# Banded attention of a two-block transformer: 64x64 scores on array halves, a standing mask in PSUM, query and gate tiles paired per step

## The reference

```python
def sink_softmax(sc, sink):
    m = jnp.maximum(jnp.max(sc, axis=-1, keepdims=True), sink)
    e = jnp.exp(sc - m)
    return e / (jnp.sum(e, axis=-1, keepdims=True) + jnp.exp(sink - m))
...
    valid = jnp.concatenate([jnp.ones((NC, N_META), dtype=bool),
                             jnp.repeat(band_chunk >= 0, CHUNK, axis=1)], axis=1)
    sr = jnp.einsum('bnqkgd,bnskd->bnkgqs', qr, kb).astype(jnp.float32) * scale
    sr = jnp.where(valid[None, :, None, None, None, :], sr, -jnp.inf)
    pr = sink_softmax(sr, sink[None, None, :, :, None, None])
    orr = jnp.einsum('bnkgqs,bnskd->bnqkgd', pr.astype(v.dtype), vb).reshape(B, S, D_MODEL)
...
def swa_layer(x, norm_g, w_in, w_out, sinks, k_sh, v_sh, cos, sin):
    B, L, _ = x.shape
    q, gate = jnp.split(rms_norm(x, norm_g) @ w_in, 2, axis=-1)
    q = partial_rope(q.reshape(B, L, B_Q_HEADS, B_HEAD_DIM), cos, sin)
    o = swa_sink_attention(q, k_sh, v_sh, sinks)
    return x + (o * jax.nn.silu(gate)) @ w_out
```

## Time and profile before

| | us |
|---|---|
| three runs | 3123.31, 3130.84, 3141.76 (median 3130.84) |
| the profiled execution's own time | 3129.51 |
| its span | 3127.7 |

### The profile page before, as it was taken

The page is one execution under the profiler, slowest core; times in us unless marked ns, Lnnn a source line. Parts: engine busy times, 40 slices in busy tenths (PEclk is TensorE's granted clock), DMA queues, the critical chain, the costliest instruction groups (busy, mean ns, idle before and its releaser), DMA issues.

```text
span 3127.7 us, 58205 instructions
## 1 busy us (share of the span) xinstructions
PE 2875.6 (92%) x23908; PEld 2721.0 (87%) x23908; DVE 950.0 (30%) x1275; ACT 1166.1 (37%) x1302; POOL 1898.5 (61%) x786
## 2 busy tenths in 40 slices
PE   6999999988898899899898989899988999999997
PEld 6889998987777678799788888899988999999996
DVE  3322232153212211221436363632514213031222
ACT  3433344333333333354424242424334434343442
POOL 4565666655343337466636364647874888888784
PEclk9999999998888779899999999999998999999998
DMA  4444444433232225454434343435653666666563
GB/s 165 134 134 117 138 146 123 140 117 110 80 95 71 70 74 176 127 150 135 138 96 127 96 127 96 122 109 156 196 174 103 188 183 188 189 180 189 177 188 116
DMA packets 119996, 425.21 MB, mean 136 GB/s; under 512 B 12672, under 2 KB 18944, under 8 KB 119552
## 3 DMA queue, kind: packets, MB, share of 16 engines
q1 hardware_dynamic: 115104, 416.53, 44.8%
q10 hardware_dynamic: 4704, 5.77, 0.6%
HBM read 418.05 MB, written 4.19 MB: 135 GB/s over the span
## 4 chain that ended last, share of the span: by engine, by line
issue 38%; PE 33%; POOL 26%; DVE 2%; ACT 0%; POOLq 0%; DMA 0%; DVEq 0%; ACTq 0%; SPq 0%
POOL wl L2085 26%; PE ps L216 9%; PE ps L223 9%; PE ps L214 9%; PE ps L234 2%; PE ps L1403 1%; DVE og L329 1%; PE ps L1832 0%; PE ps L1839 0%; PE ps L1834 0%; DVE xT L321 0%; ACT wh L195 0%; POOLq L2088 0%; DVE hl L1867 0%; DVE arena L315 0%
## 5 line engine op out<-in xcount | busy, mean ns | idle before, releaser
L2085 POOL TENSOR_TENSOR wl<-raw,wh 128x1024 fp32r<-128x1024 f32 x782 | 1898.3, 2449 | 1195.1 <-ACT wh L195 1194.4
L195 ACT ACTIVATE wh<-raw 128x2048 fp32r<-128x2048 f32 x391 | 747.4, 1912 | 842.0 <-PE ps L223 491.8
L214 PE MATMUL ps<-hh,wh 128*128 128x256 f32 (+1 forms) x3568 | 906.0, 291 | 54.1 <-DVE hl L257 42.8
L216 PE MATMUL ps<-hl,wh 128*128 128x256 f32 (+1 forms) x3568 | 898.9, 289 | 0.0
L214 PEld LDWEIGHTS ps<-hh,wh 128*128 128x128 f32 x3568 | 689.8, 193 | 61.0 <-issue 43.8
L216 PEld LDWEIGHTS ps<-hl,wh 128*128 128x128 f32 x3568 | 692.0, 194 | 0.7
L223 PE MATMUL ps<-hh,wl 128*128 128x256 f32 (+1 forms) x3568 | 469.8, 284 | 0.0
L223 PEld LDWEIGHTS ps<-hh,wl 128*128 128x128 f32 x3568 | 449.0, 190 | 0.2 <-POOL wl L2085 0.2
L214 PE MATMUL ps<-gh,wh 128*128 128x256 f32 x1536 | 395.2, 295 | 0.3 <-ACT wh L195 0.3
L216 PE MATMUL ps<-gl,wh 128*128 128x256 f32 x1536 | 389.7, 292 | 0.0
L214 PEld LDWEIGHTS ps<-gh,wh 128*128 128x128 f32 x1536 | 310.3, 202 | 3.0 <-ACT wh L195 0.5
(11 more groups left out here) (296 smaller groups left out, 2450.5 us busy)
## 6 DMA issues: line engine op xcount, KB each, us to landing
raw<-weights SPq DMA_DIRECT2D x782, 512.0 KB, 3.6
xT<-tokens SPq DMA_DIRECT2D x1, 2176.0 KB, 8.6
spill<-xT ACTq DMA_DIRECT2D x1, 2048.0 KB, 7.5
xT<-spill ACTq DMA_DIRECT2D x1, 2048.0 KB, 10.0
out<-xT SPq DMA_DIRECT2D x1, 2048.0 KB, 7.5
C<-consts SPq DMA_DIRECT2D x1, 1984.0 KB, 12.0
arena<-lora ACTq DMA_DIRECT2D x4, 384.0 KB, 3.1
P<-params SPq DMA_DIRECT2D x1, 125.0 KB, 12.8
```

Source lines behind the costliest of these rows:

```text
L195: nc.scalar.activation(wh[:, m % 2, :, :].rearrange("p a b -> p (a b)"), raw[:, 2 * (m % 2):2 * (m % 2) + 2, :, :].rearrange("p a b c -> p ...
L214: nc.tensor.matmul(acc[0:m, 0:n], wh[:, slot, kt, 0:m], rh[:, kt, 0:n], start=(kt == kts[0]), stop=False)
L216: nc.tensor.matmul(acc[0:m, 0:n], wh[:, slot, kt, 0:m], rl[:, kt, 0:n], start=False, stop=False)
L2085: nc.gpsimd.tensor_tensor(wl[:, s // 2, h, :], raw[:, s, :, :], wh[:, s // 2, h, :].bitcast(F32), ALU.subtract)\
```

## The change

- **Scores.** Each head's 64 queries of a chunk are multiplied with exactly the keys that they may see, on half the array: weights 64 x 64 (one chunk of queries of one head), five column ranges (80, 144, 208, 16 and 192 keys) for each of the two heads, ten products a step. Queries of even chunks go to partitions 0 to 63 of the output, of odd chunks to 64 to 127; head a writes bank 2 + a. Keys lie with the meta keys first.
- **Mask.** The places of banks 2 and 3 that no product writes are filled with -1e30 once, by five VectorE fills before the loop. The mask products and the zeroed key array go; `kd` is one copy of the keys in each half.
- **Values.** `turn_kv` turns the values in blocks of 64 keys into both halves of the partitions, 20 products, after the first query tile.
- **Steps.** 16 steps, all written out, each with one query tile (of the next step) and one gate tile; the gate tile is cut into six parts (`part`), four ahead of the transposes and two behind. Eight transposes instead of ten; one ScalarE copy `wx` and one VectorE copy `w2` take the turned weights out of PSUM. P·V is five blocks of keys for each head, ten products of 64 x 64 weights. The output bank alternates (4 + s % 2), as do q and gb.
- **Rotation** of the queries: 256 columns per step, between the scaling of the probabilities and the copy `w2`.
- **Split** of the outputs: three quarters inside the steps 5 to 14, the fourth behind.
- The order of weight tiles in DRAM follows.

```diff
+        def part(pe, phase_name, t, k, acc, rh, rl, n):
+            q = FIRST[phase_name] + t
+            slot = q % 2
+            if k == 0:
+                pe.wait_ge(hi_done, q + 1)
+            if k < 4:
+                for kt in range(4 * k, 4 * k + 4):
+                    nc.tensor.matmul(acc[:, 0:n], wh[:, slot, kt, :], rh[:, kt, 0:n], start=(kt == 0), stop=False)
+                    ins = nc.tensor.matmul(acc[:, 0:n], wh[:, slot, kt, :], rl[:, kt, 0:n], start=False, stop=False)
+            else:
+                pe.wait_ge(lo_done, 2 * q + k - 3)
+                for kt in range(8 * (k - 4), 8 * (k - 4) + 8):
+                    ins = nc.tensor.matmul(acc[:, 0:n], wl[:, slot, kt, :], rh[:, kt, 0:n], start=False,
+                                           stop=(kt == 15))
+            return ins
...
+        f2 = carve([("pair", PAIR), ("kd", 4, NT), ("v2", 5, 256), ("q", 2, 256), ("sh", 256), ("xc", 256),
+                    ("p0", 6, 64), ("p1", 10, 64), ("wx", 512), ("w2", 512), ("gb", 2, 256), ("stb", 32),
+                    ("kv", 4, NT), ("ksh", 2, NT)])
...
-            nc.vector.memset(fb["kd"], 0.0)\
-                .then_inc(V.sem, V.step("zero"))
-            dve.wait_ge(V.sem, V.at("zero"))
-            for g in range(4):
-                for h in range(2):
-                    nc.vector.tensor_copy(fb["kd"][64 * h:64 * h + 64, g, NT * h:NT * h + NT],
-                                                 fb["kv"][64 * (g % 2):64 * (g % 2) + 64, g // 2, :])\
-                        .then_inc(V.sem, V.step(f"k{g}_{h}"))
+            dve.wait_ge(SK["a"].sem, SK["a"].at("c3"))
+            for k, (rows, at) in enumerate((((0, 128), (0, 48)), ((0, 128), (192, 240)), ((0, 64), (128, 192)),
+                                          ((0, 64), (448, 512)), ((64, 128), (256, 320)))):
+                nc.vector.memset(ps[rows[0]:rows[1], 2:4, at[0]:at[1]], NEG)\
+                    .then_inc(V.sem, V.step(f"neg{k}"))
+            dve.wait_ge(V.sem, V.at("radd"))
+            for h in range(2):
+                for e in range(2):
+                    to = kd[64 * h:64 * h + 64].rearrange("p (a b) n -> p a b n", b=2)[:, :, e, :]
+                    of = x[64 * e:64 * e + 64]
+                    nc.vector.tensor_copy(to[:, :, META:NT], of[:, :, 0:SEQ])\
+                        .then_inc(V.sem, V.step(f"k{h}{e}"))
+                    nc.vector.tensor_copy(to[:, :, 0:META], of[:, :, SEQ:NT])\
+                        .then_inc(V.sem, V.step(f"m{h}{e}"))
...
+            for b in range(5):
+                keys = slice(64 * b - 64, 64 * b) if b else slice(NT - 64, NT)
+                for k in range(2):
+                    for a in range(2):
+                        at = 256 * (b % 2) + 128 * k
+                        ins = mm(ps[64 * a:64 * a + 64, 4 + b // 2, at:at + 128], kv[:, 2 + k, keys], c("ident"))
...
+            for s in range(STEPS_B):
+                g, ends = s // 4, s == STEPS_B - 1
+                pe.wait_ge(SQ["v"].sem, SQ["v"].at("radd", s))
+                if s:
+                    pe.wait_ge(A.sem, A.at("e3", s - 1))
+                halves = [(slice(64 * a, 64 * a + 64), 2 + a) for a in range(2)]
+                for rows, at, keys, to in ((slice(0, 64), 0, slice(0, 80), 48), (slice(64, 128), 64, slice(0, 144), 48),
+                                           (slice(0, 64), 128, slice(0, 208), 240),
+                                           (slice(64, 128), 192, slice(0, 16), 240),
+                                           (slice(64, 128), 192, slice(80, 272), 240)):
+                    for r_, b in halves:
+                        ins = quad(ps[rows, b, to + keys.start:to + keys.stop], q[r_, s % 2, at:at + 64],
+                                   kd[r_, g, keys])
...
+                if not ends:
+                    pe.wait_ge(SQ["a"].sem, SQ["a"].at("q", s))
+                    tile(pe, "b", 1 + 2 * s, 0, 0, [(ps[:, 0, :], gh, gl, ALL)], SEQ).then_inc(tile_done, 1)
+                if s:
+                    pe.wait_ge(A.sem, A.at("g", s - 1))
+                n = 2 + 2 * s - ends
+                for k in range(4):
+                    part(pe, "b", n, k, ps[:, 1, :], gh, gl, SEQ)
+
+                pe.wait_ge(V.sem, V.at("p3", s))
...
+                for k in (4, 5):
+                    ins = part(pe, "b", n, k, ps[:, 1, :], gh, gl, SEQ)
...
+                pe.wait_ge(A.sem, A.at("wx", s))
+                pe.wait_ge(V.sem, V.at("w2", s))
+                if s >= 2:
+                    pe.wait_ge(V.sem, V.at("o", s - 2))
+                o = ps[:, 4 + s % 2, 0:256]
+                for b, cols, w_ in ((0, slice(0, 256), w2[:, 256:512]), (1, slice(0, 256), wx[:, 0:256]),
+                                    (2, slice(0, 256), wx[:, 256:512]), (3, slice(128, 256), w2[:, 0:128]),
+                                    (4, slice(128, 256), w2[:, 128:256])):
                     for a in range(2):
+                        r_ = slice(64 * a, 64 * a + 64)
+                        ins = quad(o[r_, cols], v2[r_, b, 64 * g:64 * g + 64], w_[r_, :], start=(b == 0),
+                                   stop=(b == 4))
...
+            for s in range(STEPS_B):
+                ends = s == STEPS_B - 1
+                act.wait_ge(V.sem, V.at("sn", s))
...
+                nc.scalar.activation(stb[:, B_SN:B_SN + 4], stb[:, B_SN:B_SN + 4], ACT.Exp)\
+                    .then_inc(A.sem, A.step("es"))
+                if not ends:
+                    query(s + 1)
+                if s in (5, 9, 13):
+                    split_bo.quarter_act(act, SB["v"], SB["v"].at("o", s - 2), s // 4 - 1)
+                act.wait_ge(T.sem, T.at("wt", s))
+                nc.scalar.activation(f2["wx"], ps[:, 6, :], ACT.Copy)\
+                    .then_inc(A.sem, A.step("wx"))
+                n = 2 + 2 * s - ends
+                act.wait_ge(tile_done, done("b", n))
+                if s >= 2:
+                    act.wait_ge(V.sem, V.at("o", s - 2))
+                nc.scalar.activation(f2["gb"][:, s % 2, :], ps[:, 1, 0:256], ACT.Silu)\
+                    .then_inc(A.sem, A.step("g"))
+                round_weights(act, "b", n + 2)
...
+                for k in range(4):
+                    w_ = (p0 if k < 2 else p1).rearrange("p (b a) n -> p b a n", a=2)[:, :, k % 2, :]
+                    nc.vector.tensor_scalar(w_, w_, stb[:, B_RR + k:B_RR + k + 1], None, ALU.mult)\
+                        .then_inc(V.sem, V.step(f"p{k}"))
+                if s < STEPS_B - 1:
+                    rope(s + 1)
+                dve.wait_ge(T.sem, T.at("wt", s))
+                nc.vector.tensor_copy(f2["w2"], ps[:, 7, :])\
+                    .then_inc(V.sem, V.step("w2"))
+                if s in (6, 10, 14):
+                    split_bo.quarter_dve(dve, s // 4 - 1)
+                dve.wait_ge(T.sem, T.at("pv", s))
+                dve.wait_ge(A.sem, A.at("g", s))
```

326 lines of the change are left out of this document (114 added, 212 removed).

## The result

| | before, us | after, us |
|---|---|---|
| runs on the same chip, median (lowest to highest) | 3133.52 (3123.31 to 3141.76), 4 | 2968.61 (2966.87 to 2970.47), 4 |
| profiled execution, span | 3127.7 | 2964.6 |
| first scores | 735.99 | 715.44 |
| attention stage, first scores to the end of the last P·V | 406.2 | 267.9 |
| first accumulation of the output product | 1151.80 | 990.47 |

The ratio is 0.9446, with a 95% interval of 0.9396 to 0.9495 (the quotient of the two medians, 0.9474, lies inside it): 165 us less. The forecast of 2966 us and its range hold.

A forecast was written before the change was run, and what follows sets the result against it. TensorE's work in the banded attention, partly at half clock, was taken as the bound. First scores 718.7, cold start 3, steps 261 and tail 5.9 gave 988.6 against 1151.8: 163 us off 3129.5, forecast 2966 us, range 2936 to 3008.

The forecast's parts named there:

- The front: Before the attention stage: key copies, value copy and first rotation put first scores at 718.7 us (712 to 722), saving 17.
- cold first step: First step of the attention stage: 3 us more for a fallen clock.
- A step without a wait: One attention step of TensorE: scores 1.3, tiles 5.6 and 3.75, transposes 0.9, last third 1.9, P·V 1.9; 15.3 us.
- VectorE's queue: Attention steps: GpSimd holds the rotation, delaying the turned-weights copy and P·V by 0 to 2.6 us; 1.0 taken, 16.3 a step.
- Rival 1: Attention steps: VectorE is never late, 15.3 us a step, 245 us for the steps, 2947 us in all; chance 0.20.
- The clock: Attention steps: P·V and scores together for 3.2 us, not 9.3; fallen clock costed at nothing while no wait is added.
- Rival 2: Attention steps: the clock falls each step after wait and small work, 18.5 us a step, +35, 3001 us; chance 0.20.
- The sum: Up to the output product: 718.7 + 3 + 261 + 5.9 = 988.6 against 1151.8 us, 163 us saved.
- Tail: From the end of P·V to the output product's first accumulation: 5.9 us instead of 9.7, only the last quarter's split waiting.
- Rival 3: Scores and P·V: array halves don't run together, scores +1.2, P·V +1.9, 49 us in all, 3015 us; chance 0.05.
- 4: Attention steps: switching between full array and halves lets nothing overlap, 30.2 us a step, +217, 3183 us; chance 0.03.
- my "four": Attention steps on TensorE: changing the tiling mode drains the array, four times a step; no time given.

The follow-up runs named there:

- the mask experiment: The kernel before without the six mask products of a step, the mask left out of the computation: stage 306.2 us instead of 406.2, ratio 0.976.

## Why the prediction was right, and where it was right by two errors

- **The front.** 718.7 forecast, 715.44 measured. The key copies were caught by GpSimd four times, as said (2.38, 2.36, 2.53 and 2.32 us), but the value copy was done at 712.99, and the rotation behind it was held for 0.99 us once, not to the end of the next two instructions. Most of the 3.3 us is no merit of the sum: VectorE began its fills at 699.99 instead of the 702.5 taken from the profile of before, and when the kernel was profiled again the first scores came at 717.97. The turning of the values took 2.40 us; I had 4.3, "half if halves run together". The cold first step cost 2.3 against 3.
- **A step without a wait.** 15.3 forecast, 14.88 measured. The mis-sized term is the scores: 1.3 against 0.96. Tile, transposes, last third and P·V (1.91) came as taken.
- **VectorE's queue.** The mechanism and its size stand: held product, held sum, copy behind them, 2.4 us instead of 2.6, in seven of fifteen steps. The average of 1.0 a step was taken between the bounds and came out as 1.1, a guess that was met; that the late step lets the next escape was the reason given, and it is what the periods show. Rival 1 (never late) is the kernel with the rotation through PSUM: its stage of 241 stands near the 245 given for it.
- **The clock.** This step failed. I costed it at nothing "while no wait is added", and then added a wait of 2.6 us to every second or third step without costing the clock again. In six of the seven late steps P·V and the scores behind it ran at half clock in part; 10 us. Rival 2 had the mechanism, and overpriced it at 2.2 us for all 16 steps.
- **The sum.** 261 + 3 for the stage against 267.9: steps too long by 0.4 times 15, or 6 us, and a missing 10 for the clock. The stage was right to 4 us because the two errors have opposite signs, and this miss and the front's cancel again: the end of P·V was forecast for 982.7 (718.7 + 3 + 261) and came at 983.38.
- **Tail.** 5.9 forecast, 7.1 measured; the last quarter took VectorE 2.31 us, beside GpSimd, and I had 1.2; TensorE waited 0.9 us for it.
- **Rival 3** (halves don't run together, +49) and **4** (switching lets nothing overlap, +217) fall: P·V 1.91 and scores 0.96 are below the values that rest on the earlier trace rows. The rule of the Trainium skill, "TensorEngine Tiling (Array Packing)", Key Properties, that a change of the tiling mode drains the array, I weighed against the change; it spoke for it, if for anything. In the rows of the kernel before shown with the mask experiment, products of 128 rows and masks of one row alternate in the scores: two mask records between others take 0.36 us (866.08 to 866.44), four take 0.59 (867.09 to 867.68), so a record takes 0.115 and what is left, 0.13, is a cost of each group of masks, however many it holds. The trace fits the rule so far, but doesn't prove it. The removed masks made eight of them a step, the new halves make two (as the order in the kernel has it), since P·V and the next scores stand together (my "four" was a miscount). Whether the 0.13 us is a drain or a load of weights that nothing hides, no run here tells apart.
- **What the prediction didn't see** is that a part of the change it named in half a sentence, the mask, carries most of the gain: 100 us, against 165 in all. The steps' sum held it without telling: 5.8 us of scores and 1.8 of cold tile went out together.

**To carry to other kernels.** Price small matmuls by records, not columns, and add what their stretch does to the clock: the masks, of 64 columns each, cost some 39 us by themselves and 61 through the clock. Before a VectorE queue that TensorE waits for is placed beside a busy GpSimd, give its operations on two tensors an operand in PSUM, or put the one that TensorE waits for ahead of those that can be held. And when a wait is added to a sum, cost the clock after it again.

## What the runs showed of the hardware

- Two operations of 256 columns took 0.43 and 0.42 us inside a GpSimd instruction with one operand in PSUM, and 2.40 and 2.47 with both in SBUF; a negation of four numbers in SBUF 2.33 against 0.17.
- Products whose results lie in other halves of the partitions overlap even with all 128 rows of the array in use. This is the turning of the values, 40 records of 128 columns in 2.40 us or 0.06 a record, where a transpose of 128 columns on the whole array takes 0.11:

```profile
704.99 2.40 PE L251 MATMUL ps<-C,arena 128*64 128x128 f32 x40
```

- In six of the seven late steps the clock fell to half, between 0.3 us before P·V began and 1.3 us after, behind the wait of 2.4 us; in the seventh, with the same wait and the same P·V, it didn't. Behind waits of 0.3 to 0.65 us in each step it didn't fall. Why the seventh was spared I can't say: no run was made for it.
- The first layer takes up to 32 us more in some executions, of kernels of both kinds, and it is then that the granted clock from 60 to 560 us is 0.88 or 0.89 instead of 0.94. Why it is granted less there is open.
